# Four weight halves made ready around each stage boundary, and squares in the order of the banks: a change to a three-layer transformer and state-space kernel

## The reference

```
# first_block, for each layer
h = rms_norm(x, norm_w[layer, 0, 0]) * (1.0 + scale) + shift
y = mixer_ab(h, ...)            # layer 1: mixer_cd
x = x + gate * rms_norm(y, norm_w[layer, 0, 1])
h = rms_norm(x, norm_w[layer, 1, 0]) * (1.0 + scale) + shift
y = swiglu(h, ffn_w_in[layer], ffn_w_out[layer])
x = x + gate * rms_norm(y, norm_w[layer, 1, 1])
...
# second_block
x = x + 0.5 * g1 * swiglu_2(modulate(rms_norm_2(x, ...), sh1, sc1), ...)
x = x + g2 * (y_mix @ w_out)     # a convolution half and a state-space half
x = x + 0.5 * g3 * swiglu_2(modulate(rms_norm_2(x, ...), sh3, sc3), ...)
return rms_norm_2(x, final_norm)
```

## Time and profile before

| what | value |
|---|---|
| runs | 1289.57, 1292.31, 1292.54 us; median 1292.31 |
| profiled execution | 1290.95 us, its span 1289.1 us |
| PE busy | 1166.0 us, 90% |
| DVE busy | 935.4 us, 73% |
| ACT busy | 588.5 us, 46% |
| mean granted clock of PE | 0.961 |
| loads | 255 chunks of 1024 KB, median 5.5 us from issue to landing |

### The profile page before, as it was taken

How to read it: one execution, slowest core, us unless ns; L and a number is a source line. 1 busy time by engine, 2 the same in 40 slices (tenths; PEclk the granted TensorE clock), 3 DMA queues, 4 the chain that set the end, 5 groups by cost and what they waited for, 6 DMA issues and landing times.

```text
span 1289.1 us, 19982 instructions
## 1 busy us (share of the span) xinstructions
PE 1166.0 (90%) x8366; PEld 1055.4 (82%) x8366; DVE 935.4 (73%) x1630; ACT 588.5 (46%) x968; POOL 70.6 (5%) x106
## 2 busy tenths in 40 slices
PE   1698878999998986889999989999999998999997
PEld 1677557899987985689999978999979986999996
DVE  5877857888785965588987668886765956765455
ACT  0543645434354546544444463454443354544443
POOL 0000000000000000068000001000000000000000
PEclk8799899999999998989999999999999998999999
DMA  9792432877883770346799717779832362665830
GB/s 377 283 398 64 170 124 102 312 306 309 273 353 131 299 305 17 109 177 256 304 230 361 267 66 300 302 279 272 312 131 105 126 144 85 246 236 206 211 131 33
DMA packets 40810, 280.83 MB, mean 218 GB/s; under 512 B 4736, under 2 KB 5264, under 8 KB 7952
## 3 DMA queue, kind: packets, MB, share of 16 engines
q1 hardware_dynamic: 37296, 269.27, 57.4%
q0 software_dynamic: 2416, 7.92, 1.9%
q10 hardware_dynamic: 1008, 2.37, 0.6%
HBM read 277.91 MB, written 1.10 MB: 216 GB/s over the span
## 4 chain that ended last, share of the span: by engine, by line
PE 65%; DVE 21%; ACT 7%; DMA 6%; issue 1%; SPq 0%; DVEq 0%; ACTq 0%
PE PS L407 64%; DVE LO L1345 7%; DMA raw<-WS 5%; DVE raw L1335 4%; ACT HI L939 2%; DVE TMP L1404 1%; DVE HLo L1399 1%; DMA SC<-scratch 1%; ACT SC L939 1%; ACT HH L939 1%; DVE SC L1538 1%; DVE TMP L1437 1%; DVE X L1446 1%; ACT HDH L939 1%; DVE FB L1495 1%
## 5 line engine op out<-in xcount | busy, mean ns | idle before, releaser
L407 PE MATMUL PS<-HH,HI 128*128 128x256 f32 x1748 | 504.3, 289 | 24.5 <-DVE LO L1345 13.8
L407 PE MATMUL PS<-HLo,HI 128*128 128x256 f32 x1748 | 504.8, 289 | 0.9 <-DVE HLo L1399 0.3
L407 PE MATMUL PS<-HH,LO 128*128 128x256 f32 x1748 | 500.9, 287 | 0.0
L1345 DVE TENSOR_TENSOR LO<-raw,HI 128x1024 fp32r<-128x1024 f32 x340 | 403.9, 1227 | 120.5 <-ACT HI L939 120.3
L939 ACT ACTIVATE HI<-raw 128x1024 fp32r<-128x1024 f32 x340 | 339.0, 1048 | 103.9 <-PE PS L407 54.1
L407 PEld LDWEIGHTS PS<-HH,HI 128*128 128x128 f32 x1748 | 341.7, 196 | 34.9 <-DVE LO L1345 17.4
L407 PEld LDWEIGHTS PS<-HLo,HI 128*128 128x128 f32 x1748 | 341.1, 195 | 4.4 <-DVE HLo L1399 3.2
L407 PEld LDWEIGHTS PS<-HH,LO 128*128 128x128 f32 x1748 | 341.7, 195 | 3.3 <-issue 0.5
L1335 DVE CUSTOM_DVE_ANT_0 raw<-raw,CB,SM 128x1024 f32<-128x1024 f32 x168 | 210.9, 1287 | 25.3 <-DMA raw<-WS 25.1
L407 PE MATMUL PS<-HI,HDH 128*128 128x512 f32 x352 | 140.2, 398 | 0.0
L407 PE MATMUL PS<-HI,HDL 128*128 128x512 f32 x352 | 139.5, 396 | 0.0
(11 more groups left out here) (230 smaller groups left out, 1022.7 us busy)
## 6 DMA issues: line engine op xcount, KB each, us to landing
raw<-WS SPq DMA_DIRECT2D x255, 1024.0 KB, 5.5
SC<-scratch POOLq DMA_DIRECT2D x2, 1024.0 KB, 13.5
FB<-gates_out POOLq DMA_DIRECT2D x3, 512.0 KB, 4.4
SQ<-gates_out POOLq DMA_DIRECT2D x3, 512.0 KB, 9.8
X<-xT ACTq DMA_DIRECT2D x1, 1024.0 KB, 6.8
SC<-ssm POOLq DMA_DIRECT2D x2, 512.0 KB, 4.2
out<-TMP SPq DMA_DIRECT2D x2, 512.0 KB, 2.6
CB<-vecs SPq DMA_DIRECT2D x1, 512.0 KB, 6.5
```

Source lines behind the costliest of these rows:

```text
L407: return e.matmul(o, l, r, start=start, stop=stop, skip_group_check=True)
L1345: e.tensor_tensor(LO[:, s % HL, :], raw_half(j, h), HI[:, s % HL, :].bitcast(fp32), O.subtract).then_inc(*D.up(("lo", s)))
```

## The change

`first_key` becomes `first_halves`, the four halves of the first two chunks of each stage, and `next_weights(tag, n)` issues the first n of them that are not issued yet. It is called with 3 at the early boundaries where it was called with both halves of the first chunk before, with 4 at the start of `modulate` on ACT and DVE, and with 3 in f3's `add_gated` after the first rows. The last use of a feed-forward looks 3 halves ahead and no longer 2. ACT squares the even bank first, without waiting for gy, and DVE's gy of either bank waits for the square of that bank. PE's list holds the same instructions, with some waits at other places.

```diff
-        first_key = {t: (t, "in", 0) if t[0] == "f" else (t, 0) for t in ("f0", "cd", "f1", "f2", "in2", "f3")}
+        first_halves = {t: [((t, "in", j) if t[0] == "f" else (t, j), h) for j in range(2) for h in range(2)]
+                        for t in ("f0", "cd", "f1", "f2", "in2", "f3")}
...
             def modulate(tag, sh, sc):
                 high(walk.mods(sc + 8))
+                if tag != "ab":
+                    next_weights(tag, 4)
...
-                for b in (2 * qt + 1, 2 * qt):
+                for b in (2 * qt, 2 * qt + 1):
                     w.wait_ge(*P.at(("acc", name, b)))
-                    if b % 2 == 0:
-                        w.wait_ge(*D.at(("gy", tag, b)))
...
-            def next_weights(tag):
-                for half in range(2):
-                    high(walk.weight(first_key[tag], half, 0))
+            def next_weights(tag, n):
+
+                for key, half in first_halves[tag][:n]:
+                    high(walk.weight(key, half, 0))
...
-                use((tag, "dn", 10), 1, 2)
+                use((tag, "dn", 10), 1, 3)
...
             add_normed("f0", "abo", 0)
-            next_weights("f0")
+            next_weights("f0", 3)
             add_normed("f0", "abo", 1)
...
             def modulate(tag, sh):
+                if tag != "ab":
+                    next_weights(tag, 4)
                 mean(tag, 2)
...
                 for b in (2 * qt, 2 * qt + 1):
                     w.wait_ge(*P.at(("acc", name, b)))
-                    if b % 2 and normed:
+                    if normed:
                         w.wait_ge(*A.at(("sq", tag, b)))
...
                 if early:
                     new_rows(tag, 0)
-                    next_weights(tag)
+                    next_weights(tag, 3)
...
                     e.tensor_tensor(X[:, qt, :], X[:, qt, :], gy[qt], O.add).then_inc(*D.up(("x", tag, qt)))
+                    if tag == "f3" and qt == 0:
+                        next_weights(tag, 3)
```

More of the change, by code:

```diff
@@ L1241, in act @@
             add_normed("f1", "cdo", 0)
-            next_weights("f1")
+            next_weights("f1", 3)
             add_normed("f1", "cdo", 1)
@@ L1473, in linear_out, with next_weights @@
                     use((name, k // 2), k % 2, min(AHEAD, 7 - k + beyond))
-            def next_weights(tag):
-                for half in range(2):
-                    low(walk.weight(first_key[tag], half, 0))
+            def next_weights(tag, n):
+                for key, half in first_halves[tag][:n]:
+                    low(walk.weight(key, half, 0))
             def ffn(tag, later, steps, after, row):
```

## The result

The changed kernel takes 1279.09 us (median of 4 runs, 1276.17 to 1280.39) against 1292.42 of the kernel before on the same chip: ratio 0.9894, 95% interval 0.9866 to 0.9922. Run again later beside another set of kernels it had 1282.44 us, ratio 0.9920 (0.9898 to 0.9943). So it is about 1% faster, 10 to 13 us; 1281.5 was forecast. The profiled execution took 1278.52 us, its span is 1276.7 us.

A forecast was written before the change was run, and what follows sets the result against it. DVE's unbroken chain of LO and gemv was taken to bound f0, PE mostly elsewhere. Terms of 10.8 us off the profiled 1290.95 gave 1280.1; with 1.36 for the median, 1281.5 us. Own range 1278.5 to 1284, wider 1277.5 to 1288.7.

The forecast's parts named there:

- Rival (a): Lead partly lost: f0 keeps only its first stall's gain, f1's low clock stays or moves; 1285.0 us, chance 0.24.
- Rival (b): Only each stage's first stall goes, later ones return, released by ACT or a DMA; 1289.7 us, chance 0.11.
- Rival (c): Slower by the clock: boundaries that keep PE waiting longer get more low clock; 1301.9 us, chance 0.05.
- f0, 4.24 less 0.10: In f0 DVE starts its first gemv 4.24 us earlier (1.88 + 2.36), less 0.10 for half 4's HI: gain 4.14 us.
- The other estimate of the prediction: From the skill's 2.66 us table switch: HI of half 5 comes 0.8 us late, f0 gains about 3.4 us.
- f1, 3.1 + 1.56: In f1 all PE waits for LO go (3.1 us), and the low clock behind the 2.88 us stall (1.56 us).
- f2, 3.0: In f2 PE's two waits for LO go whole: gain 3.0 us, before the boundary's cost.
- f3, 1.2: In f3 PE's one wait for LO goes whole: gain 1.2 us, with no boundary cost.
- The cost of half 3 in cd and f2, 0.46 each: At these boundaries half 3's LO stands ahead of gy and delays gy of bank 3 by 0.46 us.
- In in2 1.15: At in2's boundary DVE is busy throughout, so half 3's LO lies whole on the path: cost 1.15 us.
- Half 4 in f0 and f1, 0.10: LO fits DVE's idle 1.28 us before the mean; HI ahead of ACT's square costs 0.1 us in each.
- The squares' order, 0 in f0 and f1: Squaring the even bank first leaves gy of bank 1 ending where it did: worth 0 in these stages.

The follow-up runs named there:

- e7: The changed kernel with three halves made ready early at each boundary instead of four: 1291.43 us, ratio 0.9990.
- e9: The kernel before with only ACT's silu table load moved behind the root of modulate, no half moved: 1288.04 us, ratio 0.9972.
- e10: e6 with the table load moved as in e9: 1273.95 us, ratio 0.9870.
- e4: The changed kernel with early halves for f0's boundary alone, two halves at all later boundaries, new squares order kept: 1288.99 us, ratio 0.9968.
- e1: The kernel before with only the new order of ACT's squares and DVE's waits for them, no half moved: 1293.09 us, ratio 0.9998.
- e3: The changed kernel with early halves for the feed-forwards f0 to f3 alone, cd and in2 as before: 1279.54 us, ratio 0.9893.
- e6: e5 with f2's third half moved to the start of modulate and its fourth behind dg (DVE) or the root (ACT): 1276.83 us, ratio 0.9878.
- e12: e10 run again word for word: 1275.50 us, ratio 0.9859 to the kernel before.
- e2: The changed kernel with the old order of the squares, so the early halves alone: 1281.62 us, ratio 0.9914.
- e8: The changed kernel run again word for word: 1282.44 us, ratio 0.9920 to the kernel before.
- e11: e3 with halves 3 and 4 both made ready at the start of modulate: 1281.21 us, ratio 0.9918.
- e5: e3 with the first gemv of the next chunk moved between dg and the first TMP in f0 and f1: 1277.01 us, ratio 0.9883.

## Why the prediction was right, and which terms were off

**Right in the mechanism.** DVE's lead is what counts in f0 and at the stalls, in two parts: 1.88 us of waiting for HI and two LOs. e7 has one LO (lead 1.12 us at f0's unit 1, the second one), e9 only the wait, as far as the table load makes it (1.40), the changed kernel both (4.24 at unit 1, forecast 4.24), e10 also the gemv (5.44 = 4.24 + 1.20). Rival (a) is out by e4: f0 kept 3.8 to 4.1 us. Rival (b), that the later stalls come back, is wrong for four halves but is what happens with three (e7), though it is still DVE's LO that releases them. Rival (c), slower by the clock, is out by the time. Behind cd's boundary there were 3.4 to 6.8 us of low clock whether it was longer or not (before, e1, e3 to e6, e9 to e12). But some of it is real: of the six times that PE waited 1.88 to 1.99 us ahead of the transposes, low clock began within 0.6 us of the wait's end three times (in2 in the first profile, 1.6 us lost; cd and f2 in e2, 0.3 each) and not in the other three (in2 in e2, e7 and e8); in the 6 us behind those of 1.20 to 1.75 us it never did. e11's waits of 2.00 and 2.01 us for dg had 6.8 us of it behind them, which f0 and f1 do not show in their length.

**The terms**, forecast and measured:

- f0, 4.24 less 0.10: the lead is 4.24 us to unit 2 and 4.15 at unit 14, then 3.79. At unit 15 DVE waits for a load in both kernels (2.88 us before, 3.00 after) and goes on 128.43 us behind the first matmul where it was 132.47: the load came sooner by 4.04 us, not by all of the lead. ACT's wait for the next load is longer too (1.75 us, 1.51 before). DVE's wait in the changed kernel:

```profile
334.58 1.29 DVE L1337 CUSTOM_DVE_ANT_0 raw<-raw,CB,SM 128x1024 f32<-128x1024 f32 x1 [3.00 <-DMA raw<-WS]
```

  The other estimate of the prediction, 3.4 us for f0 with HI of half 5 coming 0.8 us too late, did not come true: ACT's HI starts at 212.81, directly behind the load of 1.28 us at 211.51, and the lead is 4.24.

- f1, 3.1 + 1.56: measured 5.8 against the kernel before and 5.0 against e1 and e4 (units 5 to 21). Two mistakes. The 3.1 us of stalls were taken for the gain, though the stall at 576.59 ends when DVE is ready, so that its end moves by the whole lead: 26.49 to 22.19 us behind the first matmul, 4.30. And not all stalls went: 1.15 us stay. Low clock in the first unit of the execution shown had hidden 2 us of the first stall, as e1 shows. The clock term itself was right: behind the stall the changed kernel gains 1.51 more (-4.30 to -5.81 in the next 4 us).
- f2, 3.0: measured 3.80 (units 5 to 21 of e3 and e8, which like the kernel before had a piece of low clock in the first unit; 4.62 in the first profile, which had none). The waits of the trace, 1.24 and 1.81 us, moved the matmul they stand before by 1.39 and 2.07. A wait is listed from the end of the matmul before, 0.28 us behind its start, where without a wait the next one starts 0.12 behind it; and the start after the first one behind a wait comes 0.22 us later and not 0.12. Another 0.2 us comes at the third unit.
- f3, 1.2: 1.4 where both have the piece of low clock in the first unit (191.6 to 190.2), 2.6 for the first profile of the changed kernel, which had none (189.0), and 4.1 between e1 and e2, the one with a stall of 2.31 and low clock behind it, the other with neither.
- The cost of half 3 in cd and f2, 0.46 each: 0.49 and 0.50 (1.75 less 1.26 and 1.25). In in2 1.15: 1.00 (1.88 less 0.88). Half 4 in f0 and f1, 0.10: 0.17 (PE's wait for dg 1.05 and not 0.88).
- The squares' order, 0 in f0 and f1: e1 shows 0 there and 0.06 us in cd and f2. With half 3 it takes 0.24 us off what that costs in cd.

With the measured sizes: 3.79 - 0.17 + 5.8 - 0.17 + 3.80 - 0.50 + 1.4 - 0.49 - 1.00 = 12.5 us; the spans of the two profiles differ by 12.4. That they meet is luck. In this pair f2 gave 4.62 and f3 2.6, as neither had the low clock in its first unit that the kernel before had, and ab was 3.1 us shorter beyond its cost; against that, cd was 3.2 longer, in2 0.4, and low clock took 1.6 in in2's boundary. The forecast had 10.8: f1, f2 and f3 were under-sized by 2.0 us together, f0 over-sized by 0.5, and in2 0.15 too dear. The forecast time, 1281.5 us, lies between the two measurements of the changed kernel, 1279.09 and 1282.44.

**The clock.** The forecast let a piece of low clock go with the long stalls. In the fourteen profiles PE waited for LO within a feed-forward 11 times for 2.10 us or more, and each time a piece of 3.4 us at 1.2 GHz began 0.2 to 1.6 us after the end of the wait; of 32 waits of 1.05 to 2.03 us none had one. With four halves no wait is longer than 1.88. The Trainium skill, "TensorE: Matmul & The Clock Gate", section "HAM oscillation — how this bites in real kernels", says that waits of PE bring the low clock back and that every one pays for it. The traces agree for waits of this length, but not on the price: 1.5 us where PE is the bound behind it (as in e7's f0 and f2 and e1's f3), nothing behind the first stall of f0 and f1 (before, e1, e4), where DVE sets the end of the next. The longer boundaries showed it in three of six cases, as said above. That the wait is the cause was not tried by a wait put in alone; e7 and e9, which lengthened a stall of 2.03 us to 3.2 and got the piece, are the nearest to it.

## What to carry to other kernels

Read what an engine's early start is worth from the end of the last stall that it feeds, not from the sum of the stalls: a lead that reaches past all of them counts in full, one that ends ahead of the next only makes that one longer, and then low clock can take all of it back. Price an item moved across a boundary at each boundary by itself: here each idle time held one item, and where no stall stood behind, the item only costs. When a stall hangs on two engines' work in series, look for the idle time of both: here the table load in ACT's wait for PE gave as much lead (1.40 us) as a half (1.12).

## What the hardware showed that was not expected

- **Low clock at a stage's start** costs 1.15 us where PE binds (f3, of the kernels with early halves there: 189.0 us in the three profiles without it, the changed kernel, e2 and e6, and 190.2 in the seven with it, e3, e5, e7, e8, e10, e11 and e12) and nothing where DVE's LO binds (f1: the same 204.7 us in the changed kernel without and in e3 and e8 with it). With the gemv moved, f1 has no stall of 0.9 us or more left, and 6.8 us of low clock at its start cost e6 1.0 us against e5 there. Which it is changes from one execution to the next of the same kernel.
- **The attention stages scatter** by 6.5 (ab) and 6.8 us (cd). In cd it goes with the clock: the shortest (132.8 us) and the longest (139.6) have a mean granted clock of 0.95 and 0.89. In ab it is not so plain: the shortest (161.5) had 0.92, less than e6 with 165.2 us and 0.94; what else sets it stays open. The two of cd:

```profile
417.30:550.10 132.80, 112.34 (x778) 98.54 (x779) 89.82 (x183) 70.78 (x125) 2.53 (x4) 0.95 0.45 179
```

```profile
417.70:557.30 139.60, 118.99 (x779) 103.48 (x779) 89.96 (x183) 70.26 (x125) 2.53 (x4) 0.89 0.44 167
```

- **A table load can go far ahead of its function.** In e9, e10 and e12 the RS copy and the eight HH run under the silu table, with as many table loads as before, and the load of 1.28 us is wholly inside ACT's wait (0.59 us of that is left in f0), but for f2 of e10 and e12, where a HI takes that place first. The Trainium skill, "ScalarE: Activation LUTs", section "Table sets: the hidden batching unit", says that cheap functions such as copy and identity are in every set; the trace agrees.
